# A second tile's mixing between expert picks, with its steps spaced anew

## The reference, cut to what matters

```python
xr, gr, cq, ckv, kr, g_rnn, g_att = jnp.split(n1 @ w_in[l], IN_SPLITS, axis=-1)
hr = _rg_lru(_causal_conv(xr, ...), ...)                 # gates sigmoid(xr @ rg_wa), sigmoid(xr @ rg_wx), then a scan
y_rnn = (hr * jax.nn.gelu(gr)) @ w_rnn_out[l]
q = (_rmsnorm(cq, q_norm_g[l]) @ w_uq[l])                # 16 heads of 64 + 32 rope
kv = (_rmsnorm(ckv, kv_norm_g[l]) @ w_ukv[l])
o = _mla_attention(...)                                  # softmax over the keys before, 16 heads
mixed = jax.nn.sigmoid(g_rnn) * y_rnn + jax.nn.sigmoid(g_att) * (o @ w_attn_out[l])
h = h + mixed @ w_out[l]
# experts, per token: 8 heads x 16 best of 16384
act = jax.nn.gelu(jnp.einsum('chkd,cd->chk', u[idx], xt))
h = h + jnp.einsum('chk,chkd->cd', g * act, v[idx])
```

## Time and profile before

| | us |
|---|---|
| median of 3 runs | 1422.48 (1420.62 to 1422.99) |
| the profiled execution | 1427.83 |
| its span | 1426.0 |
| TensorE matmul busy | 1188.5 (83%) |
| VectorE busy | 886.7 (62%) |
| ScalarE busy | 508.4 (36%) |
| GpSimd busy | 287.5 (20%) |
| moved by DMA | 414.93 MB, mean 291 GB/s |

### The profile page before, as it was taken

The page is one execution under the profiler, slowest core; times in us unless marked ns, Lnnn a source line. Parts: engine busy times, 40 slices in busy tenths (PEclk is TensorE's granted clock), DMA queues, the critical chain, the costliest instruction groups (busy, mean ns, idle before and its releaser), DMA issues.

```text
span 1426.0 us, 23109 instructions
## 1 busy us (share of the span) xinstructions
PE 1188.5 (83%) x8702; PEld 795.0 (56%) x8702; DVE 886.7 (62%) x2284; ACT 508.4 (36%) x1526; POOL 287.5 (20%) x269
## 2 busy tenths in 40 slices
PE   7999998999999999999897878986666665656564
PEld 4445798987479988998675544754122222222111
DVE  7526766556563563147585487566777787777654
ACT  1214222211262143122442476324344444344334
POOL 0000000000000000001231334322354344443440
PEclk9899999999999999999998989998678778787867
DMA  8344100243324586779999999999999999999995
GB/s 314 129 150 148 47 3 3 76 158 122 119 89 131 196 301 214 238 266 399 365 421 413 394 393 379 421 420 423 413 425 425 423 426 424 424 425 426 425 425 245
DMA packets 82960, 414.93 MB, mean 291 GB/s; under 512 B 10847, under 2 KB 15327, under 8 KB 49761
## 3 DMA queue, kind: packets, MB, share of 16 engines
q0 software_dynamic: 37152, 269.50, 45.6%
q1 hardware_dynamic: 45554, 143.69, 28.4%
q10 hardware_dynamic: 144, 0.26, 0.0%
HBM read 412.36 MB, written 1.06 MB: 290 GB/s over the span
## 4 chain that ended last, share of the span: by engine, by line
PE 46%; DMA 30%; DVE 6%; issue 3%; ACT 3%; POOL 2%; POOLq 0%; DVEq 0%; ACTq 0%
DMA row<-peer_in,arena 14%; PE bank L1893 12%; DMA arena<-peer_in,arena 12%; PE bank L2915 7%; DMA ring<-stream_in 4%; PE bank L1425 3%; PE bank L1505 2%; PE bank L2803 2%; PE bank L1482 2%; PE bank L846 2%; PE bank L2081 2%; PE bank L655 1%; PE bank L645 1%; POOL arena L3235 1%; DVE arena L3193 1%
## 5 line engine op out<-in xcount | busy, mean ns | idle before, releaser
L2915 PE MATMUL bank<-arena 128*64 128x512 f32 x808 | 321.6, 765 | 153.1 <-ACT arena L3050 153.1
L3193 DVE CUSTOM_DVE_ANT_0 arena<-arena 128x1024 f32<-128x1024 f32 x202 | 246.6, 1224 | 153.7 <-DMA arena<-peer_in,arena 150.8
L3235 POOL DMA_INDIRECT arena<-peer_in,arena x202 | 219.7, 1088 | 561.3 <-PE bank L2915 371.2
L2915 PEld LDWEIGHTS bank<-arena 128*64 128x64 f32 x808 | 76.5, 160 | 323.1 <-issue 319.7
L1893 PE MATMUL bank<-arena,ring 128*128 128x128 f32 (+1 forms) x1984 | 239.8, 281 | 13.3 <-DMA ring<-stream_in 11.7
L1893 PEld LDWEIGHTS bank<-arena,ring 128*128 128x128 f32 x1984 | 232.2, 194 | 27.6 <-issue 14.5
L3034 ACT ACTIVATE arena<-arena 128x2 f32<-128x2 f32 (+1 forms) x130 | 26.4, 203 | 393.6 <-DVE arena L3193 393.5
L3038 ACT ACTIVATE arena<-arena 128x1 f32<-128x1 f32 x256 | 85.4, 380 | 4.3
L3043 ACT ACTIVATE arena<-arena 128x1 f32<-128x1 f32 x256 | 84.1, 375 | 6.8 <-DVE arena L3199 6.4
L2803 PEld LDWEIGHTS bank<-arena,ring 128*128 128x128 f32 x512 | 65.8, 209 | 34.6 <-issue 29.3
L2915 PE MATMUL bank<-row,arena 128*64 128x512 f32 x112 | 71.5, 774 | 7.1 <-ACT arena L3050 7.1
(11 more groups left out here) (395 smaller groups left out, 1856.6 us busy)
## 6 DMA issues: line engine op xcount, KB each, us to landing
ring<-stream_in SPq DMA_DIRECT2D x243, 512.0 KB, 4.7
ring<-stream_in SPq DMA_DIRECT2D x16, 384.0 KB, 5.6
arena<-peer_in,arena POOLq DMA_INDIRECT x202, 19.9
row<-rows_in SPq DMA_DIRECT2D x4, 512.0 KB, 18.2
ring<-stream_in SPq DMA_DIRECT2D x16, 128.0 KB, 7.4
cst<-cst_in SPq DMA_DIRECT2D x1, 1900.0 KB, 17.0
row<-rows_in POOLq DMA_DIRECT2D x2, 512.0 KB, 6.0
cst<-rg_w_in SPq DMA_DIRECT2D x1, 1024.0 KB, 6.7
```

The costliest lines, as they stand in the source:

```text
L2915: return nc.tensor.matmul(core.banks[2 * t + b][rows_of(j), :], diag[i % ND], places[seat[i]][:, D + b * 512:D + (b + 1) * 512], start=Fal ...
L3193: ins = nc.vector.tensor_tensor_reduce(out=row, in0=row, in1=X2[t][i % 2], scale=STEEP, scalar=0.0, op0=ALU.mult, op1=ALU.add, accum_out=d ...
L3235: pool.indirect_dma_start(out=places[seat[i]], out_offset=None, in_=g.names["peer"], in_offset=bass.IndirectOffsetOnAxis(ap=index[:, i:i + ...
```

## The change

The second tile's portions are reordered on three engines; the arithmetic stays.

1. On TensorE the first `gr` quad and the gates stand before the low-rank panels `cq`, `ckv` and `kr`, so before the first pair of picks; the sums of squares and the wait for the keys' rope stand later. ScalarE's and VectorE's portions follow. As they would still read the recurrence's buffers, the squares and the rope's part of the second tile get room in `r`, which isn't in use there.
2. In the attention steps, mask and reciprocal stand one and two picks earlier on VectorE, exponential and divide one and two picks earlier on ScalarE, keep one earlier; scores stand one earlier, turn and weigh where they were. There is one step more.
3. The second tile's mixing fills two banks of four panels instead of eight, and VectorE adds each bank in one instruction.
4. `GATED` is 10 instead of 16, `LATER` 96 instead of 112; a few numbers behind names change with the places.

In the diff the steps of TensorE come first, then those of ScalarE (`i - 4` to `i - 3`), then those of VectorE.

```diff
+    LOW = plan("r")
+    Q_SQ, KV_SQ, KR_PART = [T1[0], LOW[:, 0:QT * P]], [T2[0], LOW[:, QT * P:(QT + CT) * P]], [AA[0], LOW[:, (QT + CT) * P:]]
...
+        def mix_quad(quad):
+            key = ("mix", quad, 1)
+            bank = claim(pe, key)
+            for m in range(4 * quad, 4 * quad + 4):
+                for k in range(0, KT, 2):
+                    pe.wait_ge(mixed_ready[1].handle, mixed_ready[1].at(k // 2 + 1))
+                single("mix", m, 1, tiles(SHARE[1], P), KT, bank, m % 4 * P, P, key, m % 4 == 3)
+                yield 1.0
...
             yield from recurrent_in(1, 1)
-            yield from queries_low(1)
-            yield from wide_panels("ckv", 1, CT)
-            yield from wide_panels("kr", 1, 2)
-            yield ("kr", 1), 3
-            squares_low(1)
-            yield 0.6
             yield from quad("gr", 1, 0, tokens[1])
-            pe.wait_ge(kr_ready[1].handle, kr_ready[1].at(1))
             for n in range(2):
                 pe.wait_ge(convolved[1].handle, convolved[1].at(n + 1))
                 gates_in(1, n)
                 yield 1.0
+            yield from queries_low(1)
+            yield from wide_panels("ckv", 1, CT)
+            yield from wide_panels("kr", 1, 2)
             yield from quad("gr", 1, 1, tokens[1])
+            squares_low(1)
+            yield 0.6
...
-            yield ("rg", 1, 1, 1), 9
+            yield ("rg", 1, 1, 1), 11
...
-            for i in range(H + 9):
+            for i in range(H + 10):
...
-                if 5 <= i < H + 5:
-                    turn(i - 5, 1, 6 + (i - 5) % 2)
+                if 6 <= i < H + 6:
+                    turn(i - 6, 1, 6 + i % 2)
...
-                if i >= 9 and i % 2:
-                    j = (i - 9) // 2
-                    weigh(j, 1, 2)
+                if i >= 10 and i % 2 == 0:
+                    weigh((i - 10) // 2, 1, 2)
...
-            yield ("att", 3, 1), 3
-            for m in range(KT):
-                mix(m, 1)
-                yield 1.0
+            yield ("att", 3, 1), 4
+            for n in range(2):
+                yield from mix_quad(n)
...
-                if 4 <= i < H + 4:
-                    divide(i - 4, 1)
-                    lay_meta(i - 4, 1)
+                if 3 <= i < H + 3:
+                    divide(i - 3, 1)
+                    lay_meta(i - 3, 1)
...
-            for i in range(H + 12):
-                yield ("step", min(i, H + 8)), max(0, i - H - 8)
-                if 1 <= i < H + 1:
-                    mask(i - 1, 1)
-                if 3 <= i < H + 3:
-                    divide(i - 3, 1)
+            for i in range(H + 10):
+                yield ("step", i), 1
+                if i < H:
+                    mask(i, 1)
+                if 1 <= i < H + 1:
+                    divide(i - 1, 1)
...
-    GATED, LATER = 16, 112
+    GATED, LATER = 10, 96
```

More of the change, by code:

```diff
@@ L1936, in squares_low @@
             for j in range(QT):
-                mm = nc.tensor.matmul(bank[:, 0:P], cst("ones"), T1[t][:, j * P:(j + 1) * P], start=j == 0, stop=j == QT - 1)
+                mm = nc.tensor.matmul(bank[:, 0:P], cst("ones"), Q_SQ[t][:, j * P:(j + 1) * P], start=j == 0, stop=j == QT - 1)
             mm.then_inc(*full(("ss_q", t)))
@@ L1943, in squares_low @@
             for j in range(CT):
-                mm = nc.tensor.matmul(bank[:, 0:w], cst("ones"), T2[t][:, j * w:(j + 1) * w], start=j == 0, stop=j == CT - 1)
+                mm = nc.tensor.matmul(bank[:, 0:w], cst("ones"), KV_SQ[t][:, j * w:(j + 1) * w], start=j == 0, stop=j == CT - 1)
             mm.then_inc(*full(("ss_kv", t)))
@@ L2211, in squares_low @@
             w = P if name == "cq" else WIDE[t]
-            count, spare, done = (QT, T1[t], q_squared[t]) if name == "cq" else (CT, T2[t], kv_squared[t])
+            count, spare, done = (QT, Q_SQ[t], q_squared[t]) if name == "cq" else (CT, KV_SQ[t], kv_squared[t])
             bank = filled(act, (name, t))
@@ L2368, in second_pass @@
                 open_in(1, n, 1)
-            yield ("rg", 1, 1, 1), 6
+            yield ("rg", 1, 1, 1), 4
             decays(1)
-            yield ("rg", 1, 1, 1), 8
+            yield ("cq", 1), 2
+            squares_low(1, "cq")
+            yield ("ckv", 1), 2
+            squares_low(1, "ckv")
+            yield ("rg", 1, 1, 1), 7
             half_root(1)
@@ L2556, in add_mixed, with add_mixed_quad @@
             nc.vector.tensor_scalar(g.n2[t][:, m, :], x[:, m, here], vec("norm2", m), None, ALU.mult).then_inc(*g.gained[t].up())
+        def add_mixed_quad(quad):
+            key, js = ("mix", quad, 1), slice(4 * quad, 4 * quad + 4)
+            bank = filled(dve, key)
+            nc.vector.scalar_tensor_tensor(out=x[:, js, P:T], in0=tiles(bank[:, :], P), scalar=0.5, in1=x[:, js, P:T], op0=ALU.mult, op1=ALU.add)\
+              .then_inc(*free(key))
+            copied(dve, key)
+            for m in range(4 * quad, 4 * quad + 4):
+                nc.vector.tensor_scalar(g.n2[1][:, m, :], x[:, m, P:T], vec("norm2", m), None, ALU.mult).then_inc(*g.gained[1].up())
         def first_pass():
@@ L2639, in second_pass @@
             for n in range(4):
-                yield ("q2", n, 1), 2
+                yield ("q2", n, 1), 1
                 rotate_queries(1, n)
-            for i in range(H + 12):
-                yield ("step", min(i, H + 8)), max(0, i - H - 8)
+            for i in range(H + 10):
+                yield ("step", i), 1
+                if i < H:
+                    mask(i, 1)
                 if 1 <= i < H + 1:
-                    mask(i - 1, 1)
-                if 3 <= i < H + 3:
-                    divide(i - 3, 1)
-                if i >= 12 and i % 4 == 0 and (i - 12) // 4 < 4:
+                    divide(i - 1, 1)
+                if i >= 12 and i % 4 == 0:
                     keep_out((i - 12) // 4, 1)
             for n in range(4):
-                yield ("att", n, 1), 2
+                yield ("att", n, 1), 1
                 share_attended(1, n)
-            for m in range(KT):
-                yield ("mix", m, 1), 2
-                add_mixed(1, m)
+            for quad in range(2):
+                yield ("mix", quad, 1), 1
+                add_mixed_quad(quad)
         first_pass()
@@ L3167, in front @@
             yield from g.later["dve"]
-            yield ("turn", "x", 1, 1), 3
+            yield ("turn", "x", 1, 1), 1
             scale(1)
```

35 lines of the change are left out of this document (16 added, 19 removed).

## The result

The change is slower: 1431.22 us median of 4 runs (1429.67 to 1433.87), against 1422.07 (1420.62 to 1422.99) for the kernel before, whose median came from one run more than above. The ratio is 1.0067, 95% interval 1.005 to 1.0085, so 7 to 12 us. The forecast was 1418.3, its range ended at 1424.5, and the slower rival gave 1427.6.

The account below looks back on a forecast made before the run. It took the gather's transfers at 425 GB/s as the bound, with 13.6 us missing in three gaps. Gains of 1.7 + 1.9 + 0.6 = 4.2 us off the 1422.48 us median gave 1418.3 us, range 1412.5 to 1424.5.

Parts of the forecast that it names:

- slower rival: Attention steps: VectorE's routing doesn't fit into ScalarE's time, 7.0 us a pair over 16 picks; 1427.6 us, chance 0.17.
- cost of the attention steps: Stretch from 835 to 870 us, missing 5.8 us of transfer: 5.2 us after the change, a gain of 0.6 us.
- the round between two engines: Attention steps, VectorE and ScalarE waiting in turn: 6.15 us a pair, leaving 7.2 us over 12 heads before cover.
- 2.0 us of cover: Attention steps: divide two picks earlier, turn unmoved, so TensorE no longer starts a pair late; 2.0 us gained.
- Gap A: 675 to 715 us at 370 GB/s, 5.2 us missing; earlier gates and seventh seat leave 3.5 us, gain 1.7 us.
- The new gap: Around 676 to 681 us: early gates delay the first pair and release two picks, not four; costs 2.7 us.
- the hole behind pair 8: Between 700 and 720 us: earlier gates and an earlier seventh seat close it, worth 4.4 us.
- Gap B: 780 to 795 us at 352 GB/s, 2.6 us missing; fewer blocks ahead of a pair, gain 1.9 us.
- list of signs: Signs of being right include GpSimd's wait near 770 to 790 us under 12 us, and 780 to 795 over 400 GB/s.
- The rest: Recurrent-branch moves, two-bank mixing and late seats from pick 96: cost or give nothing while the transfer queue is full.
- third sign of being wrong: A stretch after 900 us under 410 GB/s, a part the prediction counted as untouched.

Follow-up runs that it names:

- e3: The change with turn_meta in bank 6 instead of 4, so it waits for ScalarE's keep and not VectorE's mask: 1423.81 us, 1.0013 of the kernel before.
- e10: The change with VectorE's reciprocal and ScalarE's divide put back one pick later, as before: 1423.70 us, 1.0018 of the kernel before.
- e5: The change with all attention steps one pick later, new spacing kept: 1426.96 us, 1.005 of the kernel before.
- e1: The change with the attention steps spaced as before on all three engines, the rest kept: 1422.54 us, 1.0015 of the kernel before.
- e6: The change with the old spacing of the attention steps, all one pick later: 1419.08 us, 0.9995 of the kernel before.
- e11: e10 with all attention steps one pick later: 1421.70 us, 1.0006 of the kernel before.
- e7: The kernel before with its attention steps one pick later and nothing else: 1425.73 us, 1.0035 of the kernel before.
- e13: e6 run again, the same kernel in another series: 1421.44 us, 0.9997 of the kernel before.
- e4: The change with ScalarE's exponential ahead of its keep in each step: 1426.31 us, 1.0037 of the kernel before.
- e2: The kernel before with the new spacing of the attention steps alone: 1429.94 us, 1.006 of the kernel before.
- e12: e11 with ScalarE's keep one pick later as well: 1428.68 us, 1.005 of the kernel before.

## Why the prediction was wrong

**The cost of the attention steps failed, in sign and size.** The step read: "between +5.8 and the -8.7 of the rival", taken as a gain of 0.6 us. The ledger has -11.9. Two things were wrong in it.

First, it closed the round between two engines, VectorE and ScalarE: reciprocal, dot, coefficients, exponential, 6.15 us. It asked what the exponential waits for only as far as ScalarE's own list. But ahead of the exponential stands a keep, and a keep waits for TensorE's turn, which stands behind a pair of picks. The true round has pair, panel, turn, keep, exponential, reciprocal, dot, routing, mask, `turn_meta`: 11.3 us from pair 40 to 42, 17.6 us from pair 42 to 46, and cutting it at the mask (e3) or lengthening it by one pick (e10) gives 7.7 and 7.0 us back. The reciprocals did wait before nearly every dot, as forecast (14.4 us in 8 waits), but e3 shows that these waits alone do not carry the loss.

Second, it booked the turn's position as a pure gain of 2.0 us of cover. The new order did free TensorE of the waits for the divide, as said (4.9 us in 10 waits from 830 to 880 before; none in the totals of after). But the turn is also a producer in the loop, and moving reciprocal and exponential toward it shortened the distance from a pair to the dot that hangs on it from seven picks to five.

**A term is missing altogether: parity.** The prediction took the start of the steps, one pick earlier, as free. Because picks go in pairs, one pick moves `turn_meta` from the first to the second of two steps. By the time missing between the pairs 40 and 56, undoing it gives 7.0 us in the change (e5), 4.0 with the old spacing (e1 against e6) and 1.7 with the reciprocal put back (e10 against e11), and doing it to the kernel before costs 2.4 (e7). These are single executions; only e6's was repeated, in e13 (5.6 and 5.5). In the run times it is clear of noise only in e7, 5.0 us, most of it behind the steps. The order of TensorE around L2032 (L2034 after) shows it before any run.

**The slower rival was the right direction with the wrong mechanism.** It was priced at 7.0 us a pair over eight pairs, to 1427.6. Measured are 34.5 us over the first four pairs, 8.6 each, and then 5.3 each. Its turns of VectorE and ScalarE do carry part of the second long interval, from dot 47 to 49, but inside the loop. Its chance, 0.17, was low: "VectorE's reciprocal and dot follow each other without a wait" described the old spacing, and spoke of nothing in the new.

**Gap A was right in mechanism, off in size.** The forecast put the first pair 675.5 - 641.2 = 34.3 us after the first pick; it came after 34.2, where the kernel before has 33.2. These lines of after answer to the earlier trace rows and the first of the earlier trace rows:

```profile
657.36 1.88 PE L2865 MATMUL bank<-arena,cst 128*128 128x512 f32 x4
659.08 3.73 PE L1983 MATMUL bank<-arena,cst 128*128 128x128 f32 x32
...
665.73 1.94 PE L2934 MATMUL bank<-arena 128*64 128x512 f32 x8
```

```profile
667.93 0.93 POOL L3254 DMA_INDIRECT arena<-peer_in,arena  x1 [29.18 <-PE bank L2934]
```

The new gap ahead of pair 8 cost 2.4 us more than before (forecast 2.7), and the hole behind pair 8 gave back 3.4 (forecast 4.4). The net is 1.0, not 1.7. The new gap stood in the sum with the 6.0 us from issue to use that the trace shows. With the fixed cost of 2.0 us that the Trainium skill states (DMA: Bandwidth & Descriptors, section "Anatomy of one DMA - SWDGE") the estimate would have been 1.6 us smaller, 1.1; the measured 2.4 is nearer to the trace's.

**Gap B too.** GpSimd's longest wait there fell from 17.81 to 13.41 us, where 14 was worked out (the "under 12" in the list of signs contradicted that working, and was wrong). From 780 to 795 us 420 GB/s passed, over the 400 of the list. The gain is 1.3 us, not 1.9; a smaller hole opened at 740 to 760 us, where 393 GB/s passed: three panels, two of which wait for the ring, stand ahead of one pair.

```profile
778.46 1.86 POOL L3254 DMA_INDIRECT row<-peer_in,arena  x1 [13.41 <-PE bank L2934]
```

**The rest was costed at nothing.** Between the pairs 56 and 112 the change misses 2.2 us more. Its slice from 1000 to 1036 us moved 400 GB/s, where 413 passed before: a stretch after 900 us under 410, which the prediction counted as untouched, and its third sign of being wrong. The variants of the change miss 1.3 to 2.9 us between these pairs and it misses 4.7. e3 and e4 have its spacing and its parity and miss 1.3 and 2.3, so these two alone don't make it; it may be of that one execution, and was not followed up. Behind pair 112 it misses 0.9 us more, and this stays when the steps are undone: all variants of the change miss 16.5 to 18.3 us there, the kernel before 15.6 and its two variants 14.7 and 16.5. With one execution each and e2 at 16.5, that is barely more than their spread. In e6 it is 1.8 us, most of the 2.2 us that the gaps A and B give it (6.4 + 2.4 against 7.3 + 3.7), which may be why the good parts can't be told in the medians. What costs it was not tried; the seats opened from pick 96 on and the mixing are what differs there.

## What to carry to other kernels

Where three engines run fixed lists against each other, a consumer's distance is not a cost of two neighbours: follow the wait through every engine until it comes back to where it began, count how many picks further on that is, and add up the round with everything queued in it (here routing and a panel, too). Check at which of two paired steps a rare operation lands; a shift by one position cost 5.0 us here with nothing else changed (e7), beside 8.4 for the spacing (e2). And a consumer placed later is not always slack: it also holds its bank longer (e12).

## What the runs showed of the hardware

TensorE's granted clock was lower where it waited more. Between the pairs 40 and 56 it is 0.98 in the kernel before, 0.87 in the change and 1.00 in e6, for the same instructions. Pair 40 of the change ran 3.6 us at a granted clock of 0.50 (1.2 GHz), where a pair at 1.00 (2.4 GHz) takes 1.94 (665.73); TensorE had been busy for 7.3 of the 12.8 us before it. Pair 42, behind the wait of 3.68 us, ran 3.58 us at 0.53. These times are themselves part of the loop, so a wait between engines was paid somewhat more than once here. The profile of the kernel before also shows that up to 10 us of difference can lie ahead of the stage that a change touches: compare from a common event, not from the start of the span.
